# Hybrid attention and short-convolution block on one Trainium2 core: another row layout for the normalised input h, and two gate tiles placed elsewhere

## What is computed

```python
h = rmsnorm(x, norm_g)
proj = jnp.einsum('bld,dn->bln', h, w_in)
(q, k, v, f_logit, z_att, u, gate_b, gate_c, z_conv,
 m_att, m_conv) = jnp.split(proj, _split_points(), axis=-1)
log_f = jax.nn.log_sigmoid((f_logit + b_f).astype(jnp.float32))
o_att = forgetting_attention(heads(q), heads(k), heads(v), log_f)
y_att = jnp.einsum('blc,cd->bld', o_att * jax.nn.silu(z_att), w_att_o)
o_conv = gate_b * short_conv(gate_c * u, conv_w)
y_conv = jnp.einsum('blc,cd->bld', o_conv * jax.nn.silu(z_conv), w_conv_o)
merged = jax.nn.sigmoid(m_att) * y_att + jax.nn.sigmoid(m_conv) * y_conv
return x + jnp.einsum('bld,de->ble', merged, w_out)
```

## Time and profile before

| | us |
|---|---|
| median of 3 runs | 1246.53 |
| lowest and highest | 1245.70, 1247.28 |
| the profiled execution's own time | 1245.82 |
| its span, first to last instruction | 1244.1 |
| TensorE busy | 1227.9 |
| VectorE busy | 758.4 |
| ScalarE busy | 572.3 |

### The profile page before, as it was taken

One profiled execution on the slowest core, in us unless ns is written; L12 is line 12 of the kernel. 1 busy time (PEld: TensorE's weight loads), 2 busy tenths in 40 slices (PEclk: granted clock), 3 DMA queues, 4 the chain that ended last, 5 costly groups with the idle time before them and its releaser, 6 DMA issues.

```text
span 1244.1 us, 19616 instructions
## 1 busy us (share of the span) xinstructions
PE 1227.9 (99%) x7481; PEld 1102.7 (89%) x7481; DVE 758.4 (61%) x826; ACT 572.3 (46%) x704; POOL 46.4 (4%) x50
## 2 busy tenths in 40 slices
PE   7999999999999999999999999999999999999997
PEld 6999999999998888889999999999999888888886
DVE  7755565656565544545777777777777654554544
ACT  7544445354345443444354544544455444443442
POOL 1000000000000000001011010110100000000000
PEclk9999999999999999999999999999999999999999
DMA  7856656666564666565465654656547466565563
GB/s 225 266 158 191 213 157 193 190 183 184 172 203 163 211 206 196 190 189 176 135 195 151 198 172 129 204 162 182 178 118 227 160 213 190 169 204 182 198 216 127
DMA packets 180193, 229.40 MB, mean 184 GB/s; under 512 B 7136, under 2 KB 140336, under 8 KB 179760
## 3 DMA queue, kind: packets, MB, share of 16 engines
q1 hardware_dynamic: 178656, 226.03, 58.7%
q10 hardware_dynamic: 1504, 2.90, 0.8%
HBM read 226.79 MB, written 2.11 MB: 184 GB/s over the span
## 4 chain that ended last, share of the span: by engine, by line
PE 97%; issue 1%; DVE 1%; DMA 0%; ACT 0%; POOL 0%; POOLq 0%; SPq 0%; ACTq 0%; DVEq 0%
PE ps L990 22%; PE ps L991 22%; PE ps L989 22%; PE ps L1003 20%; PE ps L1004 10%; DMA x_nat<-in_x 0%; PE ps L1118 0%; PE ps L983 0%; POOL rstd L391 0%; PE ps L1131 0%; PE ps L1129 0%; PE ps L1039 0%; PE ps L1128 0%; PE ps L1119 0%; PE ps L1130 0%
## 5 line engine op out<-in xcount | busy, mean ns | idle before, releaser
L593 DVE TENSOR_TENSOR w_lo<-w_raw,w_hi 128x1024 fp32r<-128x1024 f32 x417 | 507.1, 1243 | 271.0 <-ACT w_hi L417 269.4
L417 ACT CAST w_hi<-w_raw 128x1024 fp32r<-128x1024 f32 x418 | 429.7, 1050 | 359.9 <-PE ps L991 203.5
L1003 PE MATMUL ps<-h,w_hi 128*128 128x512 f32 x1024 | 361.3, 394 | 0.0
L989 PE MATMUL ps<-h,w_hi 128*128 128x258 f32 (+1 forms) x1040 | 297.1, 286 | 1.5 <-DVE w_lo L593 0.9
L990 PE MATMUL ps<-h,w_hi 128*128 128x258 f32 (+1 forms) x1040 | 297.4, 286 | 0.0
L991 PE MATMUL ps<-h,w_lo 128*128 128x258 f32 (+1 forms) x1040 | 296.7, 285 | 0.0
L1004 PE MATMUL ps<-h,w_lo 128*128 128x256 f32 x1024 | 287.8, 281 | 0.0
L1003 PEld LDWEIGHTS ps<-h,w_hi 128*128 128x128 f32 x1024 | 192.3, 188 | 42.6
L989 PEld LDWEIGHTS ps<-h,w_hi 128*128 128x128 f32 x1040 | 195.8, 188 | 2.7 <-DVE w_lo L593 1.2
L991 PEld LDWEIGHTS ps<-h,w_lo 128*128 128x128 f32 x1040 | 195.8, 188 | 0.0
L990 PEld LDWEIGHTS ps<-h,w_hi 128*128 128x128 f32 x1040 | 195.7, 188 | 0.0
(11 more groups left out here) (146 smaller groups left out, 935.5 us busy)
## 6 DMA issues: line engine op xcount, KB each, us to landing
w_raw<-in_w_in SPq DMA_DIRECT2D x322, 512.0 KB, 4.6
w_raw<-in_w_conv_o SPq DMA_DIRECT2D x32, 512.0 KB, 4.4
w_raw<-in_w_att_o SPq DMA_DIRECT2D x32, 512.0 KB, 4.6
w_raw<-in_w_out SPq DMA_DIRECT2D x32, 512.0 KB, 4.5
neg_cb<-neg_c_dram ACTq DMA_DIRECT2D x8, 272.0 KB, 3.2
x_nat<-in_x SPq DMA_DIRECT2D x4, 512.0 KB, 5.9
x_res<-in_x SPq DMA_DIRECT2D x1, 2048.0 KB, 9.6
out<-y SPq DMA_DIRECT2D x6, 256.0 KB, 2.8
```

What stands on the lines that cost most here:

```text
L417: nc.scalar.copy(w_hi[:, c % RING, :], w_raw[:, c % RAW, :]).then_inc(w_rounded, 1)
L593: nc.vector.tensor_tensor(w_lo[:, c % RING, :], w_raw[:, c % RAW, :], w_hi[:, c % RING, :].bitcast(F32), ALU.subtract).then_inc(w_split, 1)
L989: nc.tensor.matmul(dst, a_hi, b_hi, start=start, stop=False)
L1003: nc.tensor.matmul(dst, a_hi, b, start=start, stop=False)
```

## The change

The rows of h become 288 words long (1152 bytes), and h begins 64 bytes into its region. With 64 bytes of meta tokens ahead, the first real token of a row then lies at a multiple of 128 bytes. The region h grows from 34816 to 36928 bytes, misc shrinks by 2048. `prod` is gone: gate is overwritten in its place. `gate_nat` lies over the last quarter of m_lo. The slices of h by tokens, the instructions and their order are otherwise the same.

```diff
+ROW, ROW_PAD = 288, 64
...
-    region("h", 2 * KT * TOK * 4)
+    region("h", ROW_PAD + 2 * KT * ROW * 4)
...
-    region("misc", 13 * 1024)
+    region("misc", 11 * 1024)
...
-    gate_at = at["misc"]
     gate = misc("gate", [P, 2, SEQ])
-    prod = misc("prod", [P, 2, SEQ])
     merged_at = at["misc"]
     prod2 = misc("prod2", [P, 2, SEQ])
     joined = misc("joined", [P, 2, SEQ])
-    gate_nat = nc.alloc_sbuf_tensor_at("gate_nat", [P, 2, HALF], F32, offset=gate_at)
...
-    h = place("h", "h", [P, 2, KT, TOK], F32R)
+    at["h"] += ROW_PAD
+    h = place("h", "h", [P, 2, KT, ROW], F32R)
...
     m_hi = place("m", "m_hi", [P, KT, SEQ], F32R)
+    gate_nat = nc.alloc_sbuf_tensor_at("gate_nat", [P, 2, HALF], F32,
+                                       offset=at["m"] + (KT - KT // NB) * SEQ * 4)
     m_lo = place("m", "m_lo", [P, KT, SEQ], F32R)
...
-                nc.vector.tensor_tensor(prod[:], joined[:], gate[:], ALU.mult).then_inc(conv_step, 1)
+                nc.vector.tensor_tensor(gate[:], joined[:], gate[:], ALU.mult).then_inc(conv_step, 1)
                 step(5)
-                nc.vector.tensor_tensor(prod2[:], prod[:], conv_gated[:], ALU.mult).then_inc(conv_step, 1)
+                nc.vector.tensor_tensor(prod2[:], gate[:], conv_gated[:], ALU.mult).then_inc(conv_step, 1)
...
-                nc.vector.tensor_scalar(prod[:], gate[:], 1.0, None, ALU.add).then_inc(att_step, 1)
+                nc.vector.tensor_scalar(gate[:], gate[:], 1.0, None, ALU.add).then_inc(att_step, 1)
                 step(6)
-                nc.vector.reciprocal(prod2[:], prod[:]).then_inc(att_step, 1)
+                nc.vector.reciprocal(prod2[:], gate[:]).then_inc(att_step, 1)
                 step(7)
                 dve.wait_ge(free[B], count(i, 2, FREE_B["att"] + 2))
-                nc.vector.tensor_tensor(prod[:], joined[:], prod2[:], ALU.mult).then_inc(att_step, 1)
+                nc.vector.tensor_tensor(gate[:], joined[:], prod2[:], ALU.mult).then_inc(att_step, 1)
...
-                nc.vector.tensor_tensor(prod2[:], joined[:], prod[:], ALU.mult).then_inc(att_step, 1)
+                nc.vector.tensor_tensor(prod2[:], joined[:], gate[:], ALU.mult).then_inc(att_step, 1)
```

## The result

The changed kernel takes 1251.0 us (median of 7 runs, 1250.2 to 1251.5) against 1246.53 us: ratio 1.0037, 95% interval [1.0027, 1.0047]. It is slower by 4.5 us. Its profiled execution has a span of 1248.5 us, 4.4 us more than before.

The account below looks back on a forecast made before the run. TensorE, busy 1227.9 of 1244.1 us, bounds the kernel through matmul spacing. Terms +1.7, +1.0 and +0.2 sum to +2.9 us, taken as 1.9: 1245.82 becomes 1247.7, plus 0.7 for the median, 1248.4 us; range 1237 to 1257.

Parts of the forecast that it names:

- the forecast's own case: Whole kernel: operand-start differences set the pace, 1246.5 to 1249.8 us; chance 0.48, 0.31 within 0.2% and 0.17 slower.
- Part 1, difference instead of address: Row length and pad: moving start less stationary, modulo 256 bytes, sets the matmul pace; +2.9 us in sum.
- REAL, +3.4 ns a set: Wide product on real tokens: 703.4 against 700.0 ns per k's four matmuls, 512 sets, +1.7 us.
- ALL, +1.0 us: Key and value stages, 272 columns: differences become 0 and 128, 753.8 against 750.0 ns a set over 256 sets.
- CONV, +0.2 us: Stages of 258 columns: differences become 56 and 184, 718.4 against 717.6 ns a set over 256 sets.
- Natural with h, 0: Natural half stages with h stationary: average stays 1.39 us a set, so no change.
- every two k, not four: Sign to look for: set lengths inside a stage should repeat every two k instead of four.
- Taking 1.9 of 2.9 us: Sum of the layout terms: shifting sets by one matmul gave 0.8 to 2.9 us, so 1.9 was taken.
- The rule of independent ports: TensorE operand reads: independent ports would make the layout sum 0; the no-change rival, 1246.5 us, had chance 0.08.
- Parts 2 and 3 at nothing: Gate product in place and gate_nat in m_lo: 0 us, since TensorE never waits for VectorE after the start.
- Alignment of the tokens: Rival on h's 128-byte token starts: all h sets reach the quickest pace, 1236.6 to 1239.7 us; chance 0.31.
- Moved tiles: Rival on o, m and weight pieces off the 128-byte grid: they cost by themselves, 1250.4 to 1271.3 us; chance 0.13.

Follow-up runs that it names:

- all tiles moved: Kernel before with 64 bytes more behind h, so o, m and the weight rings move while rows of h stay: 1248.9 us, ratio 1.0019.
- Constant differences: Kernel before with the gate parts and 320-word rows, gate in the gaps, one operand-start difference throughout: 1237.9 us (0), 1248.4 (64), 1251.9 (128), 1250.6 (192).
- kernel wholly on the grid: Changed kernel with 192 bytes more behind h, returning o, m and the weight rings to 128 modulo 256: 1244.9 us, ratio 0.9987.
- one wholly off it: Changed kernel with 64 bytes more ahead of h and 192 behind, every operand 64 bytes off the 128-byte grid: 1244.7 us, ratio 0.9983.
- difference 0 in every row: Kernel before with the gate parts, 320-word rows of h, gate in the gaps, real tokens agreeing with the weights modulo 256: 1237.9 us, ratio 0.9934.
- The shift by 64: Kernel before with 64 bytes more behind h (1248.9 us), or with 64 bytes between m and the weight rings (1250.9 us).
- the shift by 192: Kernel before with 192 bytes between m and the weight rings, h and o left alone: 1253.0 us, one timing.

## Why the prediction was right, and where it was off

The time, 1251.0 us, lies in the range, 2.6 us above the 1248.4 forecast. The likeliest single outcome was a change within 0.2%; it was 0.37% slower, which the forecast's own case had at 0.17 of its 0.48. The mechanism held in the main; the sum, +2.9 us before it was shaded to 1.9, was too small against the measured 4.5, in CONV and in natural with h above all.

- **What bounds the kernel.** Right. TensorE's three waits are the same.
- **Part 1, difference instead of address.** Right in the main, and shown: equal differences at other addresses gave equal stages to 0.01 us, the natural half stage with o went to 21.97 and 22.40 us on demand, and it stayed at 21.78 us when both operands moved together. Two things speak against its wording. The forecast would call itself wrong where the pace changes and the differences do not, and REAL stages did just that with all tiles moved (11.28 us); and for keys it is not the starts that agree in the quickest sets.
- **REAL, +3.4 ns a set.** Measured 703.3 against 700.0: right, 1.5 us for 1.7.
- **ALL, +1.0 us.** Measured 0.8 us. The forecast's own averages had 752.5 ns for keys with equal starts, among the longest sets; that spoke against equal starts as the quick case and was listed under a rival, but not followed up.
- **CONV, +0.2 us.** Measured 1.3 us, the largest single miss: the sets went to 728 and 718 ns, where the average of k mod 4 = 0 and 2 had been 718. Constant differences of 56 and 184 cost 716 and 720 ns, so some 5 of the 723 come from alternating, a cost that the forecast did not have.
- **Natural with h, 0.** Measured 0.8 us: 1395 ns a set for 1390. Constant differences of 192 and 64 would give (1400 + 1373)/2 = 1387, so alternating between them costs some 8 ns on top. The sign "every two k, not four" held for REAL and failed here.
- **Taking 1.9 of 2.9 us.** Wrong. The worry was justified (a delay does not belong to the set in which it shows), but it was used to shade the sum down, when it ought to have widened the terms both ways. For REAL, constant differences of 64 and 192 cost 698 and 707 ns, where the sets of before had 705 and 702; that they averaged alike was luck.
- **The rule of independent ports** (the Trainium skill, SBUF — State Buffer, "Who interferes with whom"). The section gives no pace. Read as a rule for the pace, as the rival did, the measurement decides against it: between natural difference 0 and 192 lie 1360 and 1400 ns for six matmuls, with nothing else changed but padding.
- **Parts 2 and 3 at nothing.** Right: 0.9999 alone.
- **The rivals.** Alignment of the tokens: out, since neither kernel wholly on the grid nor one wholly off it stands apart. Its price was real, though: 1236.6 to 1239.7 us had been worked out for all sets at the quickest pace, and difference 0 in every row gives 1237.9. That the sum fits is partly luck: it had 3.8 us from natural with h and 3.0 or more from REAL, and the 8.4 us are 3.6 there, 1.0 in REAL, 2.8 in ALL and 0.7 in CONV. Moved tiles: out as put (no cost by themselves), but moving only one of two operands is just what costs.

**What stays open.** Why moving the other tiles alone made REAL stages 11.28 us with the same four differences. The shift by 64 brings it in two kernels and the shift by 192 does not, so the pattern's place against the unit of four k counts; that the semaphore wait at the start of each unit is the reason was only argued, and no run separates the two. Nor is it shown whether the start or the end of the moving operand counts. Nor do the runs say what in the hardware the 256 bytes are.

## What to carry to other kernels

When TensorE is never waiting, compare stages with the same matmul by time per matmul; a few ns of difference times thousands is the whole remaining gain. Lay the stationary and the moving operand so that their relative place modulo 256 bytes is the same, and the quick one, in every row (here: the real tokens agree with the weights, also for keys, which begin 64 bytes ahead), which asks for row lengths that are a multiple of 256 bytes; and when one region grows, look at where every region behind it lands, because here 192 unused bytes more were worth 6 us. To find space for such rows, small tiles can live in the gaps.

## What the runs showed of the hardware that was not expected

- A matmul of 512 columns follows the last by 226.7 ns when the stationary and the moving start agree modulo 256 bytes, and by 229 (natural difference 64), 232.3 (128) or 233.3 ns (192) otherwise, natural stages all; a shift of every operand by 64 bytes changed no stage by more than 0.01 us. For 272 columns (six matmuls a set) the quickest start difference was 192 and not 0: 740 against 752 ns.
- A stream of matmuls can keep two paces with the same instructions: 693 or 706 ns for a set of four, chosen by what ran before, and a break of one transpose moved it from the one to the other (one timing).
